# Memory attention of the second layer woven into the score levels of gated linear attention

## The chip, the cores and the metric

The kernel runs on one core of one Trainium2 chip (trn2). The metric is device time in microseconds (us) of one execution; lower is better. The program is written instruction by instruction: each engine (TensorE for matmuls, VectorE, ScalarE, GpSimd, and SyncE for DMA) runs its own list in order and waits on semaphores for the others.

## What is computed

The reference is one inference step of a two-layer decoder trunk, for one prompt of 256 tokens and for 8 batches of 4 sampled tokens (32 columns), so that activations are 288 columns wide. Layer 0 mixes tokens by native sparse attention, layer 1 by gated linear attention (GLA). Each layer also attends with 4 heads into 256 memory tokens, the prompt into keys and values computed here, each sampled batch into its own cached ones, and is followed by a squared-ReLU MLP. The part the change is about, for head h:

```python
def memory_attention(q, k, v, g_q, g_k):        # q (L, 128) of one head; k, v (256, 128)
    q = q * rsqrt(mean(q * q) + eps) * g_q      # norm of each query, gains per element
    k = k * rsqrt(mean(k * k) + eps) * g_k
    s = q @ k.T * 128 ** -0.5
    p = exp(s - max(s)); p = p / sum(p)
    return p @ v
```

In GLA the scores between tokens of a prompt are q(i) . k(j) times a decay exp(-sum of gates between j and i), per element of a 192-wide head. They are computed by levels: at level n, blocks of 2**n tokens are split in their middle, both factors are written relative to that middle, and a mask keeps the pairs whose common block has this size.

## The kernel before, in words

`linear_layer` (L2816) runs stages one after another; each is a block in which every engine has a list, and a block begins when all engines have ended the one before. Its stages are: the input projection, `prepare_linear`, `score_levels`, `linear_outputs` (L2476), then for the memory `normalize_queries` (L2719), `attend_memory_prompt` (L2757, which calls `attend_prompt`, L1370) and `attend_memory_sampled` (L2051), then `finish_linear` (L2667), after which the output projection follows.

`score_levels` (L2337) has 9 steps: levels 0 to 7, and a last one (CROSS, 8) for the pairs of the two halves of 128 tokens. For each level VectorE subtracts the decays (`diff`, L2377) two levels ahead, ScalarE takes Abs and Exp in place (L2424, L2426), VectorE multiplies the queries (L2387) and GpSimd the keys (L2436), TensorE multiplies the 4 heads (L2471), VectorE masks the result out of PSUM (L2399) and GpSimd adds it to `att` (L2444). A head of 192 elements takes two matmuls per product, one of 128 rows and one of 64. Every operand is float32, which TensorE runs in two passes, so the profile counts two records per matmul. Levels 0 to 2 also have the 32 sampled columns. The last step's copy is L2394.

`normalize_queries` squares the memory queries, sums over a head by a matmul with ones (L2734), takes the root and the reciprocal of the whole 128x1152 tile and multiplies. `attend_prompt` works on pairs of units (head, tile of 128 queries): scores (L1444), maximum (L1494, L1496), exponential (L1540), division (L1508), transposes (L1455), copy (L1557), output (L1465). `attend_memory_sampled` loads each batch's keys and values (L2088, L2089), squares (L2144, ScalarE), sums (L2177), roots, inverts, scales the keys on GpSimd (L2098), transposes them (L2110), copies (L2162), scores the 4 heads of a batch (L2120), and after a softmax multiplies the values (L2132).

In layer 0, `attend_sampled` (L1582) streams the cached keys and values of 40 chunks through slots: 10 in the weight ring (2 of them for keys) and 12 of its own (2 for keys).

Of the kernel before, what the change touches and what calls it, by code (L numbers as in the profile page):

```python
# [24 lines left out]
P = 128  # L25
# [641 lines left out]
def memory_keys_values(nc, g, a, base, layer, next_chunks):  # L667
# [3 lines left out]
    with ExitStack() as ctx:  # L671
# [77 lines left out]
        def _(dve):  # L749
# [29 lines left out]
            nc.vector.tensor_scalar(g.mem_k[layer], banks[:, 4:8, 0:MEM_LEN], g.vec[:, gk:gk + 1], None, ALU.mult)  # L779
# [11 lines left out]
def merge(*programs):  # L791

    ahead = [(next(p, None), n) for n, p in enumerate(programs)]
    while True:
        left = [(at, n) for at, n in ahead if at is not None]
        if not left:
            return
        n = min(left)[1]
        ahead[n] = (next(programs[n], None), n)

# [781 lines left out]
def attend_sampled(nc, g, a, base, next_chunks):  # L1582

    with ExitStack() as ctx:
# [10 lines left out]
        rest = sb("keys_values", [P, 12, CHUNK_PAGES, GROUPS * HD])  # L1595
# [3 lines left out]
        for n in range(TOTAL):  # L1599
# [6 lines left out]
            slots.append((region, at_ring, key_slot, 2 + list(before).index(v)))  # L1606
# [19 lines left out]
        pair_score = sb("pair_score", [P, PAIRS, 2 * CMP_BLOCKS // 2])  # L1626
# [10 lines left out]
        o = sb("o", [P, 2, HD])  # L1637
        k_ps = ps("k_ps", [P, GROUPS, 512])
# [258 lines left out]
        def _(dve):  # L1897
# [4 lines left out]
            def front():  # L1902
# [39 lines left out]
                nc.vector.tensor_reduce(pair_score[:], small_ps[:].rearrange("p (t n c) -> p t n c", t=PAIRS, c=2),  # L1942
# [394 lines left out]
def score_levels(nc, g):  # L2337

    CROSS = LEVELS
    with ExitStack() as ctx:
# [10 lines left out]
        ps = ctx.enter_context(nc.psum_tensor("lev_ps", [P, 2, GLA_HEADS, 512], F32))  # L2356
        diffed, distanced, exped, q_decayed, k_decayed, scored, masked, added = map(sem, (
            "diffed", "distanced", "exped", "q_decayed", "k_decayed", "scored", "masked", "added"))
# [8 lines left out]
        def blocked(ap, level):  # L2367
            return ap.rearrange("p k (n c) -> p k n c", c=2 ** level)

        @block.vector  # L2370
        def _(dve):
# [18 lines left out]
            def mask(level):  # L2390
                dve.wait_ge(scored, level + 1)
                src = ps[:, level % 2]
                if level == CROSS:
                    nc.vector.tensor_copy(g.att[:, :, 1], src[:, :, 0:P]).then_inc(masked, 1)  # L2394
                    return
# [3 lines left out]
                last = nc.vector.tensor_tensor(  # L2399
                    g.att[:, :, 0:3:2] if level == 0 else masked_to[level % 2],  # L2400
                    src[:, :, 0:SEQ].rearrange("p h (t i) -> p h t i", t=QT),
                    m.unsqueeze(1).unsqueeze(1).to_broadcast([P, GLA_HEADS, QT, P]), ALU.mult)
                if level in few_levels:
                    last = nc.vector.tensor_tensor(
                        g.att[0:SAMPLED, :, 3, 0:SAMPLED] if level == 0 else few[:, level % 2],
                        src[0:SAMPLED, :, SEQ:TOKENS],
# [3 lines left out]
            diff(1)  # L2410
            diff(2)
            for level in range(CROSS + 1):
                if level + 1 <= CROSS:
                    queries(level + 1)
                if level + 3 <= CROSS:
                    diff(level + 3)
                mask(level)

        @block.scalar
        def _(act):  # L2420
            for level in range(1, CROSS + 1):
                f = factor[level % 2][:, :, 0:span(level)]
                act.wait_ge(diffed, level)
                nc.scalar.activation(f, f, ACT.Abs).then_inc(distanced, 1)  # L2424
                act.wait_ge(distanced, level)
                nc.scalar.activation(f, f, ACT.Exp, scale=-1.0 / GATE_TAU).then_inc(exped, 1)  # L2426

        @block.gpsimd
        def _(pool):
# [20 lines left out]
            for level in range(1, CROSS + 1):  # L2450
                keys(level)
                if level >= 2:
                    add(level - 1)

        @block.tensor
        def _(pe):
            for level in range(CROSS + 1):
                lq, lk = (q, k) if level == 0 else (decayed_q[level % 2], decayed_k[level % 2])
                wait(pe, k_decayed, level)

                wait(pe, masked, level - 1)
                spans = [(slice(0, P), slice(P, SEQ), 0)] if level == CROSS else \
                    [(slice(t * P, (t + 1) * P), slice(t * P, (t + 1) * P), t * P) for t in range(QT)]
                if level in few_levels:
                    spans.append((slice(SEQ, TOKENS), slice(SEQ, TOKENS), SEQ))
                for h in range(GLA_HEADS):
                    for keys, queries, col in spans:
                        n = keys.stop - keys.start
                        pieces = head_pieces(h)
                        for e, (t, rows) in enumerate(pieces):  # L2470
                            mm = nc.tensor.matmul(ps[0:n, level % 2, h, col:col + n], lk[rows, t, keys],  # L2471
                                                  lq[rows, t, queries], start=(e == 0), stop=(e == len(pieces) - 1))
                mm.then_inc(scored, 1)
# [245 lines left out]
def normalize_queries(nc, g, layer, first):  # L2719

    with ExitStack() as ctx:
        sem = counters(nc, ctx, f"qnorm{layer}_")
        squares = ctx.enter_context(nc.sbuf_tensor(f"qnorm{layer}_squares", [P, MEM_HEADS, TOKENS], F32))
        gain = ctx.enter_context(nc.sbuf_tensor(f"qnorm{layer}_gain", [P, 1], F32))
# [226 lines left out]
```

## Time and profile before

| | us |
|---|---|
| median of 3 timed runs (lowest, highest) | 3810.02 (3807.48, 3811.71) |
| profiled execution, its own time | 3808.96 |
| its span, first to last instruction | 3806.7 |
| score levels (first product to the last copy's end) | 2489.95 to 2583.08 |
| the three memory stages of layer 1 | 2723.16 to 2812.41 |
| mean granted clock of TensorE over the span | 0.907 |

The span is divided into stages, and a stage's cost is read from the timeline between its first and its last instruction. A matmul record's time is as modelled from the granted clock; 1.00 of the windows' clock column is 2.4 GHz, 0.50 is 1.2 GHz, and values between are mixtures over the window.

### The profile page before, as it was taken

To read this page: it belongs to the slowest core of one execution; us is meant where nothing else is said; L and a number is where in the kernel's file an instruction comes from. 1 tells how busy PE (TensorE), PEld (TensorE's weight loads), DVE (VectorE), ACT (ScalarE), POOL (GpSimd) and SP (SyncE) were. 2 spreads that over 40 slices of the span, in tenths; PEclk is the share of its full clock that TensorE was granted. 3 is DMA by queue.
4 is the path that set the end of the run, shared out by engine and by line. 5 is a ranking of instruction groups with operands and counts; after the bars stand their busy time and mean duration, and the time that the engine had idled before them with its cause. 6 is when DMAs were issued, how large, how long until landed. Compare 5 with 4: busy or idle time off the path is not lost. (4 is left out here: it accounts for less than half of the span.)

```text
span 3806.7 us, 57145 instructions
## 1 busy us (share of the span) xinstructions
PE 3392.8 (89%) x23817; PEld 3088.4 (81%) x23817; DVE 1639.3 (43%) x1879; ACT 1274.9 (33%) x1363; POOL 208.7 (5%) x131
## 2 busy tenths in 40 slices
PE   7799999676577999999999999889759999999999
PEld 5699999354244999999999999863239999999999
DVE  4543334444544354333443354344544543334433
ACT  3432323123455243333333333230143433333322
POOL 0000000002231000000000000043010000000000
PEclk9899999656787999999999999957779999999999
DMA  4545352302554545454544444203245454445454
GB/s 143 185 159 173 117 158 92 117 1 89 166 188 142 164 149 164 146 166 155 166 154 164 160 155 165 85 1 112 100 144 166 144 165 150 165 160 164 148 166 136
DMA packets 317204, 537.06 MB, mean 141 GB/s; under 512 B 18213, under 2 KB 115455, under 8 KB 316040
## 3 DMA queue, kind: packets, MB, share of 16 engines
q1 hardware_dynamic: 316376, 529.70, 42.3%
q10 hardware_dynamic: 624, 4.46, 0.3%
q8 instruction: 150, 2.46, 0.3%
q14 instruction: 54, 0.44, 0.0%
HBM read 517.23 MB, written 25.19 MB: 142 GB/s over the span
## 5 line engine op out<-in xcount | busy, mean ns | idle before, releaser
L468 DVE TENSOR_TENSOR project_weights_low<-ring,project_weights_high 128x2048 fp32r<-128x2048 f32 x344 | 788.5, 2292 | 1203.0 <-ACT project_weights_high L403 1203.0
L403 ACT ACTIVATE project_weights_high<-ring 128x2048 fp32r<-128x2048 f32 x344 | 658.6, 1915 | 1264.3 <-PE project_banks L333 1264.2
L331 PE MATMUL project_banks<-high,project_weights_high 128*128 128x288 f32 x2560 | 763.3, 298 | 44.9 <-DVE project_weights_low L458 41.0
L332 PE MATMUL project_banks<-low,project_weights_high 128*128 128x288 f32 x2560 | 761.4, 297 | 0.0
L333 PE MATMUL project_banks<-high,project_weights_low 128*128 128x288 f32 x2560 | 761.2, 297 | 0.0
L331 PE MATMUL project_banks<-up_high,project_weights_high 128*128 128x288 f32 x2048 | 609.8, 298 | 27.5 <-DVE project_weights_low L458 27.5
L332 PE MATMUL project_banks<-up_low,project_weights_high 128*128 128x288 f32 x2048 | 608.7, 297 | 0.0
L333 PE MATMUL project_banks<-up_high,project_weights_low 128*128 128x288 f32 x2048 | 608.5, 297 | 0.0
L331 PEld LDWEIGHTS project_banks<-high,project_weights_high 128*128 128x128 f32 x2560 | 488.1, 191 | 47.3 <-DVE project_weights_low L458 42.6
L332 PEld LDWEIGHTS project_banks<-low,project_weights_high 128*128 128x128 f32 x2560 | 487.8, 191 | 0.0
L333 PEld LDWEIGHTS project_banks<-high,project_weights_low 128*128 128x128 f32 x2560 | 486.6, 190 | 0.0
L331 PEld LDWEIGHTS project_banks<-up_high,project_weights_high 128*128 128x128 f32 x2048 | 390.1, 190 | 28.4 <-DVE project_weights_low L458 28.4
L332 PEld LDWEIGHTS project_banks<-up_low,project_weights_high 128*128 128x128 f32 x2048 | 389.8, 190 | 0.0
L333 PEld LDWEIGHTS project_banks<-up_high,project_weights_low 128*128 128x128 f32 x2048 | 388.7, 190 | 0.0
L331 PE MATMUL project_banks<-project_high,project_weights_high 128*128 128x288 f32 x1088 | 322.6, 297 | 15.8 <-DVE project_weights_low L458 14.7
L333 PE MATMUL project_banks<-project_high,project_weights_low 128*128 128x288 f32 x1088 | 322.8, 297 | 0.0
L332 PE MATMUL project_banks<-project_low,project_weights_high 128*128 128x288 f32 x1088 | 322.3, 296 | 0.0
L949 PE MATMUL cmp_hid_ps<-cmp_blocks,ring 128*128 128x128 f32 (+1 forms) x2048 | 241.8, 276 | 0.0
L949 PEld LDWEIGHTS cmp_hid_ps<-cmp_blocks,ring 128*128 128x128 f32 x2048 | 236.4, 192 | 0.0
L331 PEld LDWEIGHTS project_banks<-project_high,project_weights_high 128*128 128x128 f32 x1088 | 206.0, 189 | 16.7 <-DVE project_weights_low L458 15.2
L332 PEld LDWEIGHTS project_banks<-project_low,project_weights_high 128*128 128x128 f32 x1088 | 206.1, 189 | 0.0
L333 PEld LDWEIGHTS project_banks<-project_high,project_weights_low 128*128 128x128 f32 x1088 | 205.9, 189 | 0.0
(422 smaller groups left out, 3347.2 us busy)
## 6 DMA issues: line engine op xcount, KB each, us to landing
ring<-in_w_up_dram SPq DMA_DIRECT2D x128, 1024.0 KB, 5.2
ring<-in_w_down_dram SPq DMA_DIRECT2D x128, 1024.0 KB, 5.1
ring<-in_gla_w_in_dram SPq DMA_DIRECT2D x40, 1024.0 KB, 5.0
h<-in_cache_nsa_kv_dram SPq DMA_DIRECT2D x256, 128.0 KB, 2.2
ring<-in_w_out_dram SPq DMA_DIRECT2D x32, 1024.0 KB, 5.1
ring<-in_nsa_w_in_dram SPq DMA_DIRECT2D x28, 1024.0 KB, 5.0
sp_keys_values<-in_cache_nsa_kv_dram SPq DMA_DIRECT2D x80, 256.0 KB, 3.5
ring<-in_w_mem_kv_dram SPq DMA_DIRECT2D x16, 1024.0 KB, 5.8
```

The source lines that it names most:

```text
L331: nc.tensor.matmul(bank, w_high, moving_high[:, kt], start=(kt == 0), stop=False)
L332: nc.tensor.matmul(bank, w_high, moving_low[:, kt], start=False, stop=False)
L333: mm = nc.tensor.matmul(bank, w_low, moving_high[:, kt], start=False, stop=(kt == k_tiles - 1))
L403: nc.scalar.activation(weights_high[:, c % 2], g.ring[:, c % RING], ACT.Copy).then_inc(rounded, 1)
L468: nc.vector.tensor_tensor(weights_low[:, c % 2], g.ring[:, c % RING], weights_high[:, c % 2].bitcast(F32), ALU.subtract).then_inc(split, 1)
L949: mm = nc.tensor.matmul(hid_ps[:, b % 2, m * HIDE_COLS:m * HIDE_COLS + hide_cols(b)], w1[:, j, m * P:(m + 1) * P], blocks[:, b % 2, j, 0:h ...
```

## The change

The three memory stages of layer 1 and their blocks are taken out. The same attention is issued inside the block of `score_levels`: each engine's list is a merge of two generators, which yield positions; the piece with the lower position is issued first. Memory positions (1 to 8 for the 8 units, 10.5 + hb/2 for 16 half batches of keys, 19 for the finish) are scaled by 9/22 to level positions.

- The norm of the queries is no longer multiplied into them: the factor goes into the exponential as its scale per row (`rms`, 9 columns), summed by 12 matmuls of one column. The queries' gain is in the memory keys instead: `mem_k` of layer 1 gets a second factor in its scaling instruction, the cached keys get it in the copy after the transposes.
- The units have one PSUM bank each for scores (a), transposes (b) and outputs (c); the keys are turned in banks a and c by halves (2 heads), and the scores of all batches gather in bank b.
- The levels have 4 banks for products instead of 8, 2 heads to a bank, in the order 0, 2, 1, 3, and one bank for the sampled columns, whose 8 matmuls come last in levels 0 to 2. The mask is two instructions of 128x512.
- The cached keys, then the values, go through 4 stage slots of 512 KB instead of 4 each with slots of their own; all scratch is in the weight ring.
- The values' product has the values stationary (128x128) and 4 columns moving: 8 matmuls a batch.
- In layer 0, `attend_sampled` has 13 slots of its own, 3 for keys, so 5 key slots in all.

```diff
@@ memory_keys_values
-            nc.vector.tensor_scalar(g.mem_k[layer], banks[:, 4:8, 0:MEM_LEN], g.vec[:, gk:gk + 1], None, ALU.mult)
+            nc.vector.tensor_scalar(g.mem_k[layer], banks[:, 4:8, 0:MEM_LEN], g.vec[:, gk:gk + 1],
+                                    g.vec[:, gq:gq + 1] if layer in MEM_RAW else 1.0, ALU.mult, ALU.mult)
@@ attend_sampled
-        rest = sb("keys_values", [P, 12, CHUNK_PAGES, GROUPS * HD])
+        rest = sb("keys_values", [P, 13, CHUNK_PAGES, GROUPS * HD])
...
-            key_slot = used[at_ring] % 2
+            key_slots = 2 if at_ring else 3
+            key_slot = used[at_ring] % key_slots
@@ score_levels
-        ps = ctx.enter_context(nc.psum_tensor("lev_ps", [P, 2, GLA_HEADS, 512], F32))
+        ps = ctx.enter_context(nc.psum_tensor("lev_ps", [P, 2, 2, 512], F32))
+        few_ps = ctx.enter_context(nc.psum_tensor("lev_few_ps", [P, 512], F32))
...
+        memory = memory_attention(nc, g, a, ctx, 1, GLA_MEM_Q, lambda m: m * (CROSS + 1) / MEM_STEPS)
...
+            def levels():                       # VectorE
+                diff(1)
+                diff(2)
+                for level in range(CROSS + 1):
+                    yield level
...
+                    yield level + 0.5
+                    mask(level)
+            merge(levels(), memory.vector(dve))
...
+                    yield level - 1.5           # ScalarE: Abs, Exp of a level
...
+                    yield level - 0.9           # GpSimd: keys of a level
...
+                        yield level - 0.4       # GpSimd: add of the level before
...
+                    for h in (0, 2, 1, 3):      # TensorE
+                        for keys, queries, col in spans:
+                            at = h // 2 * SEQ + col
+                            mm = product(ps[:, level % 2, h % 2, at:at + P], h, keys, queries)
...
+def memory_attention(nc, g, a, ctx, layer, first, at):
...
+    def loads(sp):
+        for n in range(2 * BATCH):
+            part, b = divmod(n, BATCH)
+            if n >= STAGES:
+                if n - STAGES < BATCH:
+                    sp.wait_ge(k_turned, 2 * (n - STAGES) + 2)
+                else:
+                    sp.wait_ge(out_done, U + n - STAGES - BATCH + 1)
+            sp.dma_start(stage[:, n % STAGES], rows[b, :, :, part]).then_inc(loaded[n % STAGES], 16)
...
+        def scores(u):
+            wait(pe, exped, u)
+            nc.tensor.matmul(bank_a[:, 0:MEM_LEN], q[:, k, i * P:(i + 1) * P], g.mem_k[layer][:, k], start=True,
+                             stop=True).then_inc(scored, 1)
...
+        def turn_keys(hb):
+            b, half = divmod(hb, 2)
+            if hb == 0:
+                pe.wait_ge(exped, U)
+            if hb == 1:
+                pe.wait_ge(out_copied, U)
+            pe.wait_ge(k_scaled, b + 1)
+            wait(pe, k_copied, hb - 1)
...
+            nc.scalar.activation(to, src[:, 0:MEM_LEN], ACT.Exp, bias=stat[:, u % 4, 0:1], scale=rms[:, col:col + 1],
+                                 accum_out=stat[:, u % 4, 1:2]).then_inc(exped, 1)
...
+            for u in range(U):                  # ScalarE
+                yield at(UNIT + u + 0.2)
+                exps(u)
+                if u:
+                    yield at(UNIT + u + 0.5)
+                    copies(u - 1)
...
+            for hb in range(-5, HB):            # ScalarE
+                b, half = divmod(hb, 2)
+                yield at(at_half(hb))
+                if hb >= 0:
+                    copy_keys(hb)
+                if half and 0 <= b + 3 < BATCH:
+                    square(b + 3)
+                if not half and 0 <= b + 2 < BATCH:
+                    root(b + 2)
@@ linear_layer
-            score_levels(nc, g)
+            score_levels(nc, g, a)
             linear_outputs(nc, g, a)
-        normalize_queries(nc, g, 1, GLA_MEM_Q)
-        attend_memory_prompt(nc, g, 1, g.p, GLA_MEM_Q)
-        attend_memory_sampled(nc, g, a, 1, g.p[:, GLA_MEM_Q:GLA_MEM_Q + MEM_HEADS, SEQ:TOKENS],
-                              g.h[:, HEADS:KT, SEQ:TOKENS])
```

The lists as the two programs issue them. TensorE before, levels 3 to 5 (L2471 is the products of a level; a row ends with its number of instructions):

```order
L2471 MATMUL lev_ps<-lev_decayed 128x128 x16
L2471 MATMUL lev_ps<-h 128x128 x16
L2471 MATMUL lev_ps<-lev_decayed 128x128 x16
```

TensorE after, from level 3 (the first L2499) to level 5 (the last). L2596 is a unit's scores, L2604 its transposes, L2613 its output, L2628 the transposes of half a batch's keys, L2641 their scores:

```order
L2499 MATMUL lev_ps<-lev_decayed 128x128 x16
L2613 MATMUL mem_bank_c<-ring,mem_v 128x128 x2
L2596 MATMUL mem_bank_a<-mem_k,gla_projected 128x256
L2604 MATMUL mem_bank_b<-ident,ring 128x128 x2
L2613 MATMUL mem_bank_c<-ring,mem_v 128x128 x2
L2604 MATMUL mem_bank_b<-ident,ring 128x128 x2
L2613 MATMUL mem_bank_c<-ring,mem_v 128x128 x2
L2499 MATMUL lev_ps<-h 128x128 x16
L2628 MATMUL mem_bank_a<-ident,ring 128x128 x4
L2628 MATMUL mem_bank_c<-ident,ring 128x128 x4
L2641 MATMUL mem_bank_b<-ring 32x256 x2
```

Where two levels followed each other directly, the rest of the units now stands between levels 3 and 4, and from level 4 on the keys.

ScalarE after, around the Abs (L2446) and Exp (L2448) of level 5; before, these two instructions followed each other with nothing between levels. L2698 and L2705 are a unit's exponential and copy, L2711 the squares, L2716 the root, L2724 the copy of half a batch:

```order
L2698 ACTIVATE ring,mem_stat<-mem_bank_a,mem_stat,mem_rms 128x256
L2705 ACTIVATE ring<-mem_bank_b 128x256
L2716 ACT_TABLE_LOAD
L2716 ACTIVATE mem_ss<-mem_ss 128x8
L2446 ACTIVATE gla_projected<-gla_projected 128x6x256
L2448 ACT_TABLE_LOAD
L2448 ACTIVATE gla_projected<-gla_projected 128x6x256
L2711 ACTIVATE ring<-ring 128x1024
L2705 ACTIVATE ring<-mem_bank_b 128x256
L2716 ACT_TABLE_LOAD
L2716 ACTIVATE mem_ss<-mem_ss 128x8
```

The last unit's copy (the second L2705) stands behind the first root, a level's Abs and Exp, two table loads and a square. In the whole block ScalarE loads a table 10 times.

## Rows read from the trace of the kernel before

**Rows 1.** The page, its first section: busy time, share of the span, instructions.
```profile
PE 3392.8 (89%) x23817; PEld 3088.4 (81%) x23817; DVE 1639.3 (43%) x1879; ACT 1274.9 (33%) x1363; POOL 208.7 (5%) x131
```

**Rows 2.** Windows of the levels, the stage removed, its first loads.
```profile
2502.00:2583.00 81.00, 79.83 (x272) 56.14 (x272) 32.28 (x25) 17.80 (x12) 50.02 (x16) 0.50 0.00 1
2723.00:2813.00 90.00, 43.67 (x331) 29.51 (x331) 38.09 (x99) 32.69 (x56) 19.35 (x14) 0.73 0.26 94
2762.00:2775.00 13.00, 0.37 (x2) 0.41 (x3) 5.28 (x17) 4.79 (x6) 4.59 (x3) 0.63 0.87 317
```

**Rows 3.** Timeline of the levels: start us, us, engine, line, out<-in, [idle before].
```profile
2501.88 13.59 PE L2471 MATMUL lev_ps<-lev_decayed 128*128 128x128 f32 x48
...
2548.32 9.92 PE L2471 MATMUL lev_ps<-lev_decayed 128*128 128x128 f32 x32
...
2550.49 0.51 PEld L2471 LDWEIGHTS lev_ps<-lev_decayed 64*128 64x128 f32 x4 [0.22 <-issue]
...
2552.66 0.93 PEld L2471 LDWEIGHTS lev_ps<-lev_decayed 128*128 128x128 f32 x4 [0.22 <-issue]
...
2582.39 0.69 DVE L2394 COPY gla_att<-lev_ps 128x512 f32<-128x512 f32 x1 [2.54 <-PE lev_ps L2471]
```

**Rows 4.** Groups by line and shape, window 2440 to 2860.
```profile
L2377 DVE TENSOR_TENSOR gla_projected<-gla_decay 128x1536 f32<-128x1536 f32 x6 | 10.6, 1759 | 31.3 <-POOL h L2436 15.7 <-POOL lev_decayed L2436 15.7
L2436 POOL TENSOR_TENSOR lev_decayed<-gla_projected 128x1536 f32<-128x1536 f32 x3 | 10.3, 3418 | 0.0
...
L2424 ACT ACTIVATE gla_projected<-gla_projected 128x1536 f32<-128x1536 f32 x6 | 8.9, 1483 | 46.8 <-DVE gla_projected L2377 46.8
```

**Rows 5.** Timeline at the edges of the stage removed.
```profile
2719.91 0.46 DVE L2643 TENSOR_TENSOR gla_projected<-gla_projected,linout_swish 128x288 f32<-128x288 f32 x1
2723.16 0.15 DVE L2746 TENSOR_SCALAR qnorm_gain<-vec 128x1 f32<-128x1 f32 x1 [2.79 <-PEq L2479]
...
2805.97 5.37 PE L2132 MATMUL mem_o_ps<-ring,mem_probs 128*32 128x128 f32 x128 [0.97 <-DVE mem_probs L2196]
...
2812.70 3.36 ACT L2696 ACTIVATE gla_projected<-h 128x864 f32<-128x864 f32 x4 [8.77 <-PEq L2054]
...
2813.67 2.69 PE L2689 MATMUL fin_ps<-gla_projected,ones 128*128 128x288 f32 x10 [1.59 <-ACT gla_projected L2696]
```

**Rows 6.** Timeline of two units of the prompt's memory attention.
```profile
2740.11 1.28 ACT L1540 ACT_TABLE_LOAD   x1 [9.11 <-PEq L2721]
...
2744.66 1.06 PE L1444 MATMUL memory_s_ps<-mem_k,memory_q 128*128 128x256 f32 x2
...
2745.76 0.42 DVE L1494 TENSOR_REDUCE memory_maxima<-memory_s_ps 128x1 f32<-128x256 f32 x1 [1.64 <-PE memory_s_ps L1444]
...
2746.41 0.47 ACT L1540 ACTIVATE memory_probs<-memory_s_ps,memory_maxima 128x256 f32<-128x256 f32 x1 [1.12 <-DVE memory_maxima L1496]
...
2747.80 0.38 ACT L1557 ACTIVATE memory_turned<-memory_t_ps 128x256 f32<-128x256 f32 x1 [0.83 <-PE memory_t_ps L1455]
...
2748.32 0.64 PE L1465 MATMUL memory_o_ps<-memory_turned,mem_v 128*128 128x128 f32 x4
2748.52 0.42 DVE L1494 TENSOR_REDUCE memory_maxima<-memory_s_ps 128x1 f32<-128x256 f32 x1 [1.29 <-PE memory_s_ps L1444]
```

**Rows 7.** Timeline of one sampled batch's keys.
```profile
2774.63 1.94 PE L2110 MATMUL mem_k_ps<-ident,mem_stage 128*128 128x128 f32 x8 [12.86 <-POOL mem_stage L2098]
...
2777.71 1.05 ACT L2144 ACTIVATE mem_squares<-mem_stage 128x1024 f32<-128x1024 f32 x1
...
2778.94 0.64 PE L2120 MATMUL mem_s_ps<-mem_turned_k,mem_q 128*32 128x256 f32 x8
```

**Rows 8.** DMA issues of the window 2755 to 2815.
```profile
mem_stage<-in_cache_mem_kv_dram SPq DMA_DIRECT2D x8, 512.0 KB, 4.4
```

**Rows 9.** Timeline of ScalarE in sparse attention.
```profile
1118.68 0.68 ACT L1851 ACTIVATE sp_turned_k<-sp_k_ps,vec 128x512 f32<-128x512 f32 x1
...
1176.50 1.06 ACT L1838 ACTIVATE mem_k<-sp_keys_values 128x1024 f32<-128x1024 f32 x1 [1.69 <-DMA sp_keys_values<-in_cache_nsa_kv_dram]
```

More of the change, by code:

```diff
@@ L797, in merge @@
             return
-        n = min(left)[1]
+        at, n = min(left)
+        yield at
         ahead[n] = (next(programs[n], None), n)
+def merge(*programs):
+    for _ in ordered(*programs):
+        pass
 def page_chunks(a, g, kind, stage, loaded):
@@ L2368, in blocked, with _ @@
             return ap.rearrange("p k (n c) -> p k n c", c=2 ** level)
+        @block.sync
+        def _(sp):
+            for _ in memory.loads(sp):
+                pass
         @block.vector
@@ L2391, in mask @@
                 dve.wait_ge(scored, level + 1)
[L2392 removed]
+                src = [ps[:, level % 2, b].rearrange("p (h n) -> p h n", h=2) for b in range(2)]
                 if level == CROSS:
[L2394 removed]
+                    for b in range(2):
+                        last = nc.vector.tensor_copy(g.att[:, b:GLA_HEADS:2, 1], src[b][:, :, 0:P])
+                    last.then_inc(masked, 1)
                     return
@@ L2448, in add, with levels @@
                 last.then_inc(added, 1)
[L2450 to L2453, printed above, removed]
+            def levels():
+                for level in range(1, CROSS + 1):
+                    yield level - 0.9
+                    keys(level)
+                    if level >= 2:
+                        yield level - 0.4
+                        add(level - 1)
+            merge(levels(), memory.gpsimd(pool))
@@ L2455, in _, with levels, product @@
         @block.tensor
         def _(pe):
[L2457 to L2468, printed above, removed]
+            def levels():
+                for level in range(CROSS + 1):
+                    yield level
+                    lq, lk = (q, k) if level == 0 else (decayed_q[level % 2], decayed_k[level % 2])
+                    wait(pe, k_decayed, level)
+                    wait(pe, masked, level if level in few_levels else level - 1)
+                    spans = [(slice(0, P), slice(P, SEQ), 0)] if level == CROSS else \
+                        [(slice(t * P, (t + 1) * P), slice(t * P, (t + 1) * P), t * P) for t in range(QT)]
+                    def product(out, h, keys, queries):
@@ L2469, in _ @@
                         pieces = head_pieces(h)
                         for e, (t, rows) in enumerate(pieces):
-                            mm = nc.tensor.matmul(ps[0:n, level % 2, h, col:col + n], lk[rows, t, keys],
-                                                  lq[rows, t, queries], start=(e == 0), stop=(e == len(pieces) - 1))
-                mm.then_inc(scored, 1)
+                            last = nc.tensor.matmul(out, lk[rows, t, keys], lq[rows, t, queries], start=(e == 0),
+                                                    stop=(e == len(pieces) - 1))
```

339 lines of the change are left out of this document (282 added, 57 removed).

## The prediction

> **What bounds the kernel now.** I read the page first: TensorE is busy 89% of the span [rows 1]. A share over the whole span says nothing of a stage, so next I cut windows. In the score levels TensorE is busy 79.83 of 81 us, VectorE 32.28, ScalarE 17.80 and GpSimd 50.02, and the granted clock is 0.50, the 1.2 GHz level [rows 2]. In the memory stages that are removed TensorE is busy 43.67 of 90 us at 0.73; of these 90, 13 go by with 0.37 us of TensorE work, while the first loads run at 317 GB/s [rows 2]. The two stages look complementary: one is full on TensorE, the other nearly empty. But both are one chain: while levels run, only the other engines have room, and memory attention needs TensorE three times per unit. So I read the timeline for what a level's products cost [rows 3], the groups for what the level loop costs elsewhere [rows 4], the edges of the removed stages [rows 5], and one unit and one batch for their chains [rows 6, 7].
>
> **What is removed.** The last VectorE instruction ahead of the stages ends at 2720.37, their first starts at 2723.16, and the next stage's first ScalarE instruction starts at 2812.70 [rows 5]. The next stage would have started some 2.3 to 2.8 us after 2720.37, as theirs did. 2812.70 - 2723.16 = 89.5; I take -90.0, with the small differences between what starts first in a block.
>
> **The level products themselves.** From level 3 a level is 16 matmuls, 9.92 us [rows 3]. The weight loads of most come singly, and three times per level two are loaded together (x4 records, once of 64 and once of 128 partitions are shown): 16 - 3 = 13 steps of 0.76 us, most spaced 0.72. The rows of 64 partitions pair where one head ends with the lower half of a tile and the next head starts with an upper half. In the order 0, 2, 1, 3 this happens once, not twice, and two heads that share a bank cannot be relied on to run beside each other: 15 steps of 0.72 = 10.85, so +0.93 in each of levels 3 to 7 (+4.7) and +1.1 in the last. Levels 1 and 2 take 13.59 now [rows 3] with the sampled columns between; with them gathered, 10.85 and 8 short matmuls, some 13.0: -1.2 to -1.5 together. Level 0 starts now at a higher clock, right behind other matmuls, and would start behind a wait for squares: +1.5. Sum +6, bounds 0 (all pairs kept) and +12 (every step single).
>
> A rule of the Trainium skill bears on the keys and values here: "TensorE: Matmul & The Clock Gate", Part 3, says that matmuls of few output columns on distinct column groups of the array run concurrently. The trace agrees: 128 records of 32 columns for the values take 5.37 us, 0.042 each [rows 5], the scores of four heads 0.64 for 8 records [rows 7]. The change leaves two groups for the scores and none for the values, so the rule speaks against it; by it the values alone would cost four times 5.37, by column count four moving columns instead of 128 take most of it back.
>
> **What is added, by gaps.** In the new list TensorE runs a level and then a few memory pieces, each of which waits for another engine, so the block gets longer by the gaps between levels. ScalarE is the engine behind most of them.
>
> A unit: scores start at 2744.66 and end 1.06 later at the slow clock, the maximum starts at 2745.76 (0.42), the exponential at 2746.41 (0.47, and reading its sum 0.19), a copy of the transposes 0.38, an output 0.64 to 1.06 [rows 6]. Before, a unit starts every 2.76 (2745.76 to 2748.52) with two in flight. Now there is one bank of each kind, and the copy of unit u-1 stands behind the exponential of unit u: scores 1.06, to the end of the exponential 1.25 and 0.3 for its sum, copy 0.38, output 0.9: 3.9, say 4.0 (3.0 at full clock).
>
> - Ahead of level 0: square of 128x1152 on ScalarE and 12 matmuls of one column: 3.1.
> - After level 0 (scores, scores, transposes): 1.06 + 1.6 + 1.06 + 0.7 and hand-overs = 4.7.
> - After levels 1 and 2: two outputs more than whole units, 8.9 and 9.3, each near 2.3 periods.
> - After level 3: the last pieces of three units 6.2, then the last output, whose copy on ScalarE stands behind root, Abs, Exp, a square and two table loads of 1.28 [rows 6]: of 2 x 1.28 + 2 x 1.48 + 1.05 + 0.2 = 6.8 [rows 4, 6, 7] some 5.8 is open. 12.0.
> - A half batch: 4 transposes at the slow clock are half of 1.94 to 1.97 for eight records, times two records each and so 1.0 to 1.5; a copy of 512 columns 0.68 [rows 9]; scores on two column groups 0.3 to 0.6. With the ends of the waits 2.4. ScalarE has per level 5 x 0.68, 2.5 x 1.05 and 2 x 1.48 + 2 x 1.28 = 11.5 beside them, a little under level and gap together. So level 4 (three and a half of them): 9.6; level 5: 12.6; level 6: 11.3; level 7, two and a half left: 4.3.
> - Tail behind the last level: transposes, copy (some 1.7), 64 matmuls of 4 columns, 128 records. No row has their shape: 32 stationary columns take 0.042 each [rows 5], 128 moving ones 1.94 / 8 = 0.243 [rows 7]. I take 0.073, near the first since few columns move: 9.3 (ends 5.4 and 31). The value loads of batches 4 to 7 wait for slots that the products of 0 to 3 free and land 4.4 us later [rows 8], which opens 3 us more: 14.0 (10.1 to 36).
>
> Together 3.1 + 4.7 + 8.9 + 9.3 + 12.0 + 9.6 + 12.6 + 11.3 + 4.3 + 14.0 = 89.8. Bounds: all pieces ready when TensorE comes to them (their own matmul time only: 43.67 of the removed stages [rows 2], dearer by the lost column groups: some 55) and, above, each of the 8 gaps and the tail 2.5 us longer, 112 (and 22 more by the tail's far end, which I give next to no weight). I keep 89.8: the nearest row is the unit's, and it is a chain.
>
> What of it lies beside the levels: the loads, squares, sums and scalings (1.05 ScalarE, GpSimd scaling) and the unit norms; what lies on the path is above. The level loop's other side, subtraction 1.76, Abs and Exp 2 x 1.48, keys 3.42 [rows 4], fits in level plus gap, about 20 us, so no level waits for its operands.
>
> **The rest.** Clock: with gaps between them the levels may be granted 1.00 in places, as units were (0.73 over the removed stages [rows 2]); half a level saved, -5, bounds 0 and -25 (five levels at half their time). The next stage: its first matmuls took 2.69 for 10 [rows 5] right behind other TensorE work; behind `linear_outputs` and a barrier they start slower, +2.3 (bounds 0, +5). Five key slots: ScalarE waits for key loads before its squares here and there (1.69 before that at 1176.50 [rows 9], eight such waits, 7.7 in all), two of them really for value slots; at most -5.1, I take -3.5, and 0 if the loads are limited by the queue. The second factor in `mem_k`'s scaling is free: same instruction; above, 0.2.
>
> Sum: -90.0 + 6 + 89.8 - 5 + 2.3 - 3.5 = -0.4. Against the profiled execution's 3808.96 that is 3808.6; the median of the runs stands 1.1 higher, 3809.6. As errors of gaps with slack on the other side are more often towards overlap (a piece that was ready), I round down: 3808.
>
> **Rivals.** (1) The weave pays: TensorE finds pieces ready because ScalarE and VectorE do them during the 10 us of a level, and one or two stretches are granted the full clock. For it: VectorE is busy 32 and ScalarE 18 of 81 us [rows 2], ScalarE waits 46.8 of them for the subtraction [rows 4]. Against: only one unit is in flight. Each gap loses about one hand-over chain (2 us, 16) and the clock gives 12 instead of 5: 3808 - 23 = 3785; with more of the clock 3775.
> (2) The other side: ScalarE's list. Its Abs and Exp wait for a subtraction that waits for GpSimd's keys, and everything of memory attention behind them waits too: exponentials, copies, squares. One wait of 2 us in each of 8 gaps is +16: 3824. It decides when ScalarE's waits for the subtraction, 46.8 now, stand in the middle of memory pieces; it is harmless as long as the subtraction is done when ScalarE comes to it, which levels of 20 us instead of 10 favour.
> (3) The table loads. There are ten of 1.28 each [rows 6]; if each also has to empty ScalarE's pipe and costs as much again, and six of ten stand on the path, +8 to +13: 3819. The Trainium skill, "ScalarE: Activation LUTs", What ACT_TABLE_LOAD costs, puts such a switch at about 2.66 us, a drain and a load; row 2740.11 has 1.28 and shows nothing of a drain.
>
> **How the numbers follow.** A change of 0.2% (7.6 us) is about what a measurement of this kernel can tell. Forecast (near 3808, own range 3799 to 3819) 0.43, of which 0.08 ends faster, 0.33 within, 0.02 slower; (1) 0.30, all faster; (2) 0.18, slower; (3) 0.09, 0.02 of it within. Faster 0.38, same 0.35, slower 0.27. The range that leaves 0.1 out on each side is 3778 to 3827.
>
> **What would show it.** Between the end of one level's products and the first of the next (L2499 rows) the gaps above, 9 to 13 us in the middle; levels of 10.85 at clock 0.50; the longest gap after level 3 with ScalarE as releaser; from the block's first product to its last copy 93.1 + 6 + 89.8 - 5 = 184 us. A block under 165 says rival 1, and the windows tell whether by clock or by gaps; over 195 with ScalarE waiting for L2389 in the gaps says rival 2; ScalarE idle right at table loads says rival 3. The forecast is wrong if a level waits for its keys, or if sparse attention moves by over 5 us either way.

## The result, and where the time went

The changed kernel takes 3826.72 us (median of 6 runs, 3822.33 to 3833.15) against 3810.35 (3805.44 to 3814.05, 6 runs): a ratio of 1.0049, 95% interval 1.0038 to 1.0060. It is slower by 16 us by the medians (14 to 23 by the interval), where 3808 and no measurable change were forecast. The profiled execution took 3822.33, its span is 3820.4, 13.7 more than before. The page, where [rows 1] had 3392.8 us:

```profile
PE 3421.8 (90%) x23832; PEld 3112.3 (81%) x23832; DVE 1637.7 (43%) x1870; ACT 1282.9 (34%) x1379; POOL 196.9 (5%) x126
```

TensorE is busy for 29 us more, although the number of its instructions hardly moved. The timeline of TensorE in the changed kernel, the block's start, the gap after level 3 and the tail (L2499 is a level's products, the answer to L2471 in [rows 3]; L2683 the sampled values):

```profile
2484.21 2.63 PE L2647 MATMUL mem_bank_c<-ones,ring 128*128 128x1 f32 x16 [1.96 <-ACT ring L2752]
2486.99 10.93 PE L2499 MATMUL lev_ps<-gla_projected 128*128 128x128 f32 x32
...
2550.57 10.77 PE L2499 MATMUL lev_ps<-lev_decayed 128*128 128x128 f32 x32
2561.13 1.06 PE L2613 MATMUL mem_bank_c<-ring,mem_v 128*128 128x128 f32 x4
2561.98 1.06 PE L2596 MATMUL mem_bank_a<-mem_k,gla_projected 128*128 128x256 f32 x2
2562.83 0.63 PE L2604 MATMUL mem_bank_b<-ident,ring 128*128 128x128 f32 x2
2564.77 0.71 PE L2613 MATMUL mem_bank_c<-ring,mem_v 128*128 128x128 f32 x4 [1.30 <-ACT ring L2705]
2565.59 0.44 PE L2604 MATMUL mem_bank_b<-ident,ring 128*128 128x128 f32 x2
2571.67 1.22 PE L2613 MATMUL mem_bank_c<-ring,mem_v 128*128 128x128 f32 x4 [5.64 <-ACT ring L2705]
2572.69 10.77 PE L2499 MATMUL lev_ps<-h 128*128 128x128 f32 x32
...
2654.29 3.00 PE L2499 MATMUL lev_ps<-h 128*128 128x128 f32 x16
2657.12 0.38 PE L2673 MATMUL mem_bank_a<-ident,ring 128*128 128x128 f32 x2
2657.98 26.25 PE L2683 MATMUL mem_bank_c<-ring 128*128 128x4 f32 x128 [0.47 <-ACT ring L2705]
...
2684.86 1.19 PE L2948 MATMUL linout_o_ps<-gla_att,gla_v_rows 128*128 128x256 f32 x2 [0.63 <-PEq L2350]
```

The rows between two L2499 rows are memory pieces; a bracket is idle time, and in this gap ScalarE's L2705, the copy of a unit's transposes, ends both waits. The last but one row is the result: 128 records with 4 columns moving take 26.25 us, and TensorE is never idle in it, since the row has no break.

The windows of the same tail say at which clock (us, busy times by engine, granted clock, DMA share, GB/s):

```profile
2654.50:2658.00 3.50, 3.03 (x19) 2.07 (x18) 1.74 (x6) 1.04 (x3) 0.00 (x0) 1.00 0.36 135
2658.00:2661.00 3.00, 3.00 (x20) 3.00 (x21) 0.08 (x1) 0.00 (x0) 0.00 (x0) 0.73 0.00 0
2661.00:2670.00 9.00, 9.00 (x43) 9.00 (x44) 0.00 (x0) 0.00 (x0) 0.00 (x0) 0.50 0.54 167
```

The last level ran at 1.00, the value product started there, and the clock fell to 1.2 GHz within its first 3 us (0.73 over them is 1.4 us at 1.00 and the rest at 0.50) and stayed. PE and PEld are busy alike; that the time is the loading of 128x128 stationary values is tested below.

From ends of stages on TensorE and VectorE in both traces the balance is:

| | forecast | measured |
|---|---|---|
| up to the end of layer 1's input projection (sparse attention's slots) | -3.5 | -6.9 (2449.86 to 2443.01) |
| ahead of level 0 | +3.1 | +3.9 |
| the levels themselves, clock included | +6 - 5 | +3.6 (92.4 to 96.0) |
| the 8 gaps | +72.7 | +74.3 |
| tail behind the last level | +14.0 | +26.5 |
| stages removed | -90.0 | -89.6 |
| linear_outputs, the stage after it, the rest | +2.3 | +1.9 |
| sum | -0.4 | +13.7 |

### The profile page after: what moved, and what is told of

It is laid out like the page before. It is cut to its first block and busy times, and to the rows that moved or that the text cites. A ratio compares the mean times of both kernels' runs of the same rounds, so it can differ in the third digit from the quotient of the medians.

```text
span 3820.4 us, 57170 instructions
## 1 busy us (share of the span) xinstructions
PE 3421.8 (90%) x23832; PEld 3112.3 (81%) x23832; DVE 1637.7 (43%) x1870; ACT 1282.9 (34%) x1379; POOL 196.9 (5%) x126
## 5 line engine op out<-in xcount | busy, mean ns | idle before, releaser
L331 PE MATMUL project_banks<-up_high,project_weights_high 128*128 128x288 f32 x2048 | 610.6, 298 | 27.5 <-DVE project_weights_low L458 27.5
```

The source lines that it names most:

```text
L331: nc.tensor.matmul(bank, w_high, moving_high[:, kt], start=(kt == 0), stop=False)
```

## Experiments

All intervals are against the kernel before on the same chip. The differences from the changed kernel compare separate measurements, in which the median of the kernel before lies between 3807.75 and 3810.35; so they are good to some 3 us, and those of a single run are less sure. A name such as "tail" is the stretch from the last level's products to the first of the next stage. A line "..." in an edit stands for lines left out.

**More columns moving.** To see what a record of the value product costs:

```diff
-    mm = nc.tensor.matmul(bank_c[:, cols], stage[:, n % STAGES, t, h * HD:(h + 1) * HD],
-                          turned[:, t * P + cols.start:t * P + cols.stop],
+    mm = nc.tensor.matmul(bank_c[:, h * 64:(h + 1) * 64], stage[:, n % STAGES, t, h * HD:(h + 1) * HD],
+                          turned[:, t * P:t * P + 64],
```

> The changed kernel with 64 columns moving instead of 4 in the 64 matmuls of the sampled values (the product then means nothing; it leaves the rest alone). Theory L (a record costs what its 128x128 stationary load costs, 0.205 us at the 1.2 GHz level, whatever moves): the 128 records stay at 25 to 28 us. Rival D (TensorE waits for the value loads of batches 4 to 7): also 26, so this run does not tell D. Rival M (short matmuls cost by their moving columns plus a fixed part): 60 more columns in two passes add at least 60 x 2 / 1200 = 0.1 us a record, 13 us in all, 39.

Measured: 3811.24 in its one run, 15.5 less than the changed kernel's median, and no theory had it. Sixteen times the columns take 11.7 us less. Its timeline, then its windows:

```profile
2655.03 14.58 PE L2683 MATMUL mem_bank_c<-ring 128*128 128x64 f32 x128 [0.47 <-ACT ring L2705]
```

```profile
2650.00:2655.00 5.00, 4.33 (x27) 2.47 (x26) 1.78 (x6) 1.73 (x4) 1.14 (x1) 1.00 0.34 105
2663.00:2670.00 7.00, 6.61 (x59) 6.47 (x58) 0.29 (x1) 0.00 (x0) 0.00 (x0) 1.00 0.39 143
```

The product starts at 1.00 as before, but with 64 columns it stays there: 14.58 / 128 = 0.114 us a record, against 26.25 / 128 = 0.205. The 0.205 is a mean that holds the first 1.4 us at 1.00; a run further down has the same product at 0.50 throughout, 27.47 / 128 = 0.215. This fits one cost that scales with the clock and hardly with the moving columns. So theory L held for what a record is made of, and missed the clock.

**Fewer stationary columns.**

```diff
-                    mm = nc.tensor.matmul(bank_c[:, cols], stage[:, n % STAGES, t, h * HD:(h + 1) * HD],
+                    mm = nc.tensor.matmul(bank_c[0:32, cols], stage[:, n % STAGES, t, h * HD:h * HD + 32],
```

> The changed kernel with the first 32 columns of each head's values stationary instead of 128 (three quarters of the output are left out), 4 columns moving as before. Theory L: the load of 32 columns is a quarter, so the 128 records fall from 26.2 to between 6 and 10 us unless the value loads then show (up to 4.4 us of landing behind batch 3's slot). Rival D (waits for the loads) and rival F (a fixed time per instruction on TensorE's queue): they stay above 20.

Measured: 3810.9 in its one run. The tail of its timeline:

```profile
2665.61 1.02 PE L2683 MATMUL mem_bank_c<-ring 128*32 128x4 f32 x16 [1.86 <-DMA ring<-in_cache_mem_kv_dram]
...
2668.07 1.02 PE L2683 MATMUL mem_bank_c<-ring 128*32 128x4 f32 x16 [0.26 <-DMA ring<-in_cache_mem_kv_dram]
```

A batch's 16 records take 1.02 us, 0.064 each, under a third of 0.215 at the same low clock; now TensorE does wait for value loads. The whole product took 11 us (2658.0 to 2669.1), waits included. The stationary operand's columns are the cost; rivals D and F fall.

**Without the last four loads.** In this kernel the loads of values 4 to 7 are not issued:

```diff
-        for n in range(2 * BATCH):
+        for n in range(2 * BATCH - STAGES):
...
-            pe.wait_ge(loaded[n % STAGES], 16 * (n // STAGES + 1))
+            pe.wait_ge(loaded[n % STAGES], 16 * (BATCH // STAGES + 1))
```

> The changed kernel without the value loads of batches 4 to 7; their products read the slots as batches 0 to 3 left them. Theory L: no change, 26 us for the 128 records. Rival D (the landing of four loads of 512 KB is in the 26.2 us): 3 us or more less.

Its product, in its timeline:

```profile
2655.88 26.15 PE L2683 MATMUL mem_bank_c<-ring 128*128 128x4 f32 x128 [0.47 <-ACT ring L2705]
```

26.15 for 26.25, and 3823.74 in its one run, inside the changed kernel's range. The prediction's "which opens 3 us more" for the landing was wrong as well: a product this slow covers the loads.

**The slots alone,** on the kernel before:

```diff
-        rest = sb("keys_values", [P, 12, CHUNK_PAGES, GROUPS * HD])
+        rest = sb("keys_values", [P, 13, CHUNK_PAGES, GROUPS * HD])
...
-            key_slot = used[at_ring] % 2
+            key_slots = 2 if at_ring else 3
+            key_slot = used[at_ring] % key_slots
...
-        pair_score = sb("pair_score", [P, PAIRS, 2 * CMP_BLOCKS // 2])
...
+        pair_score = o[:].rearrange("p a d -> p (a d)").rearrange("p (t n) -> p t n", t=PAIRS)
```

> The kernel before with only the five key slots of sparse attention added. The trace of the changed kernel has attend_sampled 9.3 us shorter and the stages around it 4 longer, gated linear attention starting 6.9 earlier. Theory: the slots alone give 5 to 9 us, 3801 to 3805. Rival (the prediction's): at most 5.1 by the waits of ScalarE's squares, 3805 to 3808. Rival (run to run difference of the granted clock): nothing.

Measured: 3803.10 (11 runs) against 3808.91, ratio 0.9984, interval 0.9975 to 0.9993: 6 us, between 3 and 10. In its profile `attend_sampled` is 242.1 long instead of 253.3, the stages ahead of it 2.6 longer. The prediction's upper bound, 5.1, counted only ScalarE's waits for key loads; the stage gained 11 here (9.3 in the changed kernel). The queue of loads shows where. Waits of SyncE's queue over sparse attention in the kernel before, for key slots to be turned (L1702, L1706):

```profile
SPq L1702 <- PE sp_k_ps L1754: 45.4, 14, 6.1
SPq L1706 <- PE sp_k_ps L1754: 18.5, 4, 7.3
```

and with the slots:

```profile
SPq L1703 <- PE sp_k_ps L1755: 19.2, 5, 7.3
SPq L1707 <- PE sp_k_ps L1755: 5.6, 3, 4.3
```

63.9 us of queue waiting became 24.8. One queue issues keys and values in order, so a key load that waited for its slot also held up the value loads behind it, which no wait of ScalarE's squares names. That this is the missing half is my reading; no run separated it.

**The weave alone,** the changed kernel with four key slots (and 12 slots of its own again, although the expectation speaks of a thirteenth):

```diff
-        rest = sb("keys_values", [P, 13, CHUNK_PAGES, GROUPS * HD])
+        rest = sb("keys_values", [P, 12, CHUNK_PAGES, GROUPS * HD])
...
-            key_slots = 2 if at_ring else 3
+            key_slots = 2
```

> The changed kernel with two key slots in the ring and two of its own, four in all, as before (the thirteenth slot holds values that nothing waits for): the weave alone. The traces have the woven block 18.7 us over the blocks that it replaces; with the slots' 5 to 9 us taken off the result: 3828 to 3834. Rival (slots give nothing once the weave is there): as the changed kernel, 3826.

Measured: 3831.66 (4 runs), ratio 1.0064, interval 1.0048 to 1.0079: the weave costs 18 to 30 us, and the slots hid a part of it. `attend_sampled` is back at 252.6, and the value product at 26.22.

**Values on column groups,** as the kernel before had them, in the woven block (`own_probs` takes the place of dead scratch, zeroed by GpSimd; eight copies place the probabilities):

```diff
+            for t in range(QT):
+                for h in range(MEM_HEADS):
+                    mm = nc.tensor.matmul(bank_c[32 * h:32 * h + 32, 0:HD], own_probs[:, t, h, b],
+                                          stage[:, n % STAGES, t, h * HD:(h + 1) * HD], start=(b == 0 and t == 0),
+                                          stop=(b == BATCH - 1 and t == QT - 1), skip_group_check=True)
```

> The changed kernel with the values product as the kernel before had it: probabilities placed in zeroed blocks of 32 columns are stationary on four column groups, the values move; still through four slots, so batches 4 to 7 load behind the products of 0 to 3. Theory L (128 full stationary loads made the tail 26 us): the 128 records take 5 to 7 us of work, spread over 9 to 12 by the landing of the last loads; with eight small copies, a copy and a transposition added (2 us), the time falls by 12 to 15 us, to 3812 to 3815. Rival D: the product falls little, above 3822.

Measured: 3809.17 (10 runs, 3803.93 to 3818.59), ratio 1.0001, interval 0.9991 to 1.0010, so some 18 us under the changed kernel's ratio, more than the 12 to 15 expected. The last part of its product:

```profile
2665.66 1.08 PE L2691 MATMUL mem_bank_c<-ring 128*32 128x128 f32 x16 [4.14 <-DMA ring<-in_cache_mem_kv_dram]
2667.12 2.24 PE L2691 MATMUL mem_bank_c<-ring 128*32 128x128 f32 x32 [0.39 <-DMA ring<-in_cache_mem_kv_dram]
```

16 records of four heads take 1.08 at the slow clock, 0.068 each, and the 4.14 us wait for the fifth batch's values stands where the forecast had put 3 us for the landing. Two things changed here at once: the stationary operand has 32 columns instead of 128, and four heads stand on four column groups. The run with 32 stationary columns and no groups had 0.064 with 4 columns moving, so the narrow operand accounts for the price; that 128 moving columns cost next to nothing more may be the groups' doing, which no run separates. The product as a whole went from 26.2 to 11.0 us. The profiled execution is the slowest of its ten, and it shows a long stretch in another stage:

```profile
2776.70:2807.40 30.70, 30.70 (x54) 6.31 (x52) 11.18 (x15) 0.00 (x0) 2.01 (x2) 0.50 0.34 115
```

`linear_outputs` has here a stretch of 30.7 us at 0.50; the changed kernel has 0.76 over the same window, its clock going up and down. The stage takes 145.1 instead of 137.5. What decides it was not settled; the other profile with the values on column groups (all three edits, below) has 145.0 too, and none of the others is over 139.9.

**Abs and Exp beside the levels.**

```diff
-                    yield level - 1.5
+                    yield level - 1.0
```

> The changed kernel with Abs and Exp of each level half a level earlier in ScalarE's list, so that they run beside the products of a level and not among the memory pieces of a gap. Theory A (the longest waits in the gaps, 5.6, 2.6, 3.6 and 3.0 us, stand behind Abs, Exp and their table loads): gaps after levels 3 to 6 fall by 2 to 5 us each, 8 to 13 us in all, 3814 to 3819. Rival (subtraction and keys come late for the queries then, or the same wait moves to another piece): within 3 us of the changed kernel.

Measured: 3804.81 (10 runs), ratio 0.9991, interval 0.9981 to 1.0000: 22 us under the changed kernel, more than the 8 to 13 expected. ScalarE in the gap after level 3, in the changed kernel:

```profile
2564.34 0.37 ACT L2705 ACTIVATE ring<-mem_bank_b 128x256 f32<-128x256 f32 x1
2564.73 1.28 ACT L2716 ACT_TABLE_LOAD   x1
...
2566.03 0.21 ACT L2716 ACTIVATE mem_ss<-mem_ss 128x8 f32<-128x8 f32 x1
2566.14 1.47 ACT L2446 ACTIVATE gla_projected<-gla_projected 128x1536 f32<-128x1536 f32 x1
2567.63 1.28 ACT L2448 ACT_TABLE_LOAD   x1
2568.92 1.48 ACT L2448 ACTIVATE gla_projected<-gla_projected 128x1536 f32<-128x1536 f32 x1
2570.31 1.04 ACT L2711 ACTIVATE ring<-ring 128x1024 f32<-128x1024 f32 x1
2571.26 0.36 ACT L2705 ACTIVATE ring<-mem_bank_b 128x256 f32<-128x256 f32 x1
```

From one copy to the next 6.9 us, all of it other work of ScalarE; here TensorE waits its 5.64. With the edit the chain is short:

```profile
2562.81 0.21 ACT L2716 ACTIVATE mem_ss<-mem_ss 128x8 f32<-128x8 f32 x1
...
2562.93 1.04 ACT L2711 ACTIVATE ring<-ring 128x1024 f32<-128x1024 f32 x1
2563.87 0.36 ACT L2705 ACTIVATE ring<-mem_bank_b 128x256 f32<-128x256 f32 x1
```

The gap after level 3 falls from 11.4 to 7.2 and the one after level 6 from 12.1 to 7.5. Those after levels 4 and 5 do not fall: other waits came in, behind VectorE's copy of the last unit's output and behind GpSimd's scaling of keys, as the rival had it.

```profile
2581.35 1.11 PE L2628 MATMUL mem_bank_c<-ident,ring 128*128 128x128 f32 x4 [4.43 <-DVE h L2784]
...
2602.78 1.12 PE L2628 MATMUL mem_bank_a<-ident,ring 128*128 128x128 f32 x4 [4.46 <-POOL ring L2588]
```

All eight gaps go from 74.3 to 65.5, -8.8. The number is the expected one, but theory A holds for two gaps of four: the waits after levels 3 to 6 fell by only 2.7 us together, and most of the rest is memory pieces that ran at a higher clock. The levels gained by the clock as well: two were granted 1.00 throughout. In its windows levels 5, 6 and 7:

```profile
2586.20:2592.50 6.30, 6.30 (x36) 4.61 (x35) 2.90 (x4) 4.93 (x6) 3.17 (x2) 1.00 0.23 83
2604.80:2615.70 10.90, 10.90 (x35) 7.74 (x34) 3.53 (x4) 4.65 (x5) 6.35 (x3) 0.50 0.00 0
2623.20:2629.50 6.30, 6.30 (x35) 4.58 (x34) 1.76 (x1) 4.40 (x4) 2.23 (x1) 1.00 0.32 86
```

The same products take 6.3 us or 10.9. The sum of the levels is 86.9 instead of 96.0. Why these two levels and not the one between them got the full clock is not shown. The sampled values' product, unchanged in this run, began at 0.50 and stayed there (0.50 over 2637.2 to 2664.6):

```profile
2637.13 27.47 PE L2683 MATMUL mem_bank_c<-ring 128*128 128x4 f32 x128 [0.47 <-ACT ring L2705]
```

**Heads in order.**

```diff
-                    for h in (0, 2, 1, 3):
+                    for h in range(GLA_HEADS):
```

> The changed kernel with the heads of a level in the order 0, 1, 2, 3. Theory O (pairs of weight loads run side by side where heads follow each other in different banks, three pairs a level instead of one): a level from 3 on falls from 10.8 to 9.9 us, all of them together by 6 to 8 us, 3819 to 3821. Rival: within 2 us.

Measured: 3811.08 (10 runs), ratio 1.0004, interval 0.9992 to 1.0015: 15 to 17 us under the changed kernel. Each level of 10.8 takes 9.8, the nine together 87.3 for 96.0 (8.7, a little over the 6 to 8 expected); the whole profiled execution is 12 us shorter. That is the 9.92 of the kernel before [rows 3]. A level's weight loads (PEld) merge in three rows of four again, where the changed kernel has one, at 2555.47:

```profile
2548.05 0.51 PEld L2499 LDWEIGHTS lev_ps<-lev_decayed 64*128 64x128 f32 x4 [0.22 <-issue]
...
2550.23 0.93 PEld L2499 LDWEIGHTS lev_ps<-lev_decayed 128*128 128x128 f32 x4 [0.22 <-issue]
...
2552.83 0.51 PEld L2499 LDWEIGHTS lev_ps<-lev_decayed 64*128 64x128 f32 x4 [0.23 <-issue]
```

The order changes both which half tiles are neighbours and which neighbours share a bank; no run tells these two apart. The remaining few us of the time are not explained; two of the ten runs were at 3797.

**All three.**

> The three edits of these runs together (values moving on four column groups, Abs and Exp half a level earlier, heads in the order 0 to 3). If they add up: 26 to 36 us less than the changed kernel, 3791 to 3801, and faster than the kernel before. If one hides another's gain (a shorter level leaves ScalarE less cover): 3802 to 3808.

Measured: 3787.82 (5 runs, 3782.80 to 3791.37), ratio 0.9946, interval 0.9932 to 0.9959: 15 to 26 us faster than the kernel before, 39 less than the changed kernel and under the 3791 to 3801 that were expected. The block is 163.1 long from first level to the next stage, against 197.9. The single gains (18, 22 and 16, together 56) are more than this. In the traces the levels take 78.9 instead of 96.0, the gaps 68.0 instead of 74.3, the tail 16.2 instead of 27.6, and `linear_outputs` 145.0 instead of 137.5. By how much the single gains share the clock's part was not taken apart.

**The product kept warm.** 64 columns again, now so that the product is right: those of a head pair move, the four that count are copied out of four banks.

```diff
+                to, pair = b % 2 * 256 + h * 64, h // 2 * 64
...
+                    mm = nc.tensor.matmul(value_banks[b // 2][:, to:to + 64], stage[:, n % STAGES, t, h * HD:(h + 1) * HD],
+                                          turned[:, t * P + pair:t * P + pair + 64],
```

> The changed kernel with the values product computed for 64 probability columns (those of a pair of heads) instead of the 4 of the batch, into four PSUM banks; the 4 that mean something are copied out. Theory C (with 4 columns the granted clock falls 1.4 us into the product, with 64 it stays at 1.00, and a record costs its stationary load at that clock): 128 records in 14 to 15.5 us, the time 10 to 14 us under the changed kernel, 3812 to 3816. Rival (the single run with 64 columns was luck of the clock): the product at 0.2 us a record or more, 26 us, no gain.

Measured: 3812.45 (10 runs), ratio 1.0007, interval 0.9998 to 1.0017: 14 us under the changed kernel by the medians (16 by the ratios), as theory C had it. Its product takes 14.9 us in all; its first half:

```profile
2659.42 3.79 PE L2685 MATMUL mem_bank_c<-ring 128*128 128x64 f32 x32 [0.47 <-ACT ring L2707]
2663.04 3.74 PE L2685 MATMUL mem_bank_b<-ring 128*128 128x64 f32 x32
```

**Warm product with the other two edits.**

> Wide values product, Abs and Exp half a level earlier, heads in the order 0 to 3. If the product stays at 1.00: 14.6 us in place of the 12 that the column groups took with waits, but a warm stage behind it (137 to 140 us instead of 145): 3784 to 3790, level with or under the run of all three. Rival (the clock at the tail depends on where the levels end): the product at 26 us, 3796 or more.

Measured: 3797.83 (6 runs, 3789.86 to 3807.42), ratio 0.9967, interval 0.9954 to 0.9979. The median is the rival's outcome; the fastest run reaches 3789.86. Only the slowest of the six, 3807.42, has a profile:

```profile
2638.29 7.09 PE L2685 MATMUL mem_bank_c<-ring 128*128 128x64 f32 x32 [0.47 <-ACT ring L2707]
2645.17 7.03 PE L2685 MATMUL mem_bank_b<-ring 128*128 128x64 f32 x32
```

```profile
2633.00:2638.00 5.00, 4.04 (x18) 2.85 (x18) 2.96 (x6) 0.81 (x3) 3.03 (x2) 0.64 0.24 91
2645.00:2655.00 10.00, 10.00 (x49) 10.00 (x48) 0.77 (x8) 0.00 (x0) 0.00 (x0) 0.50 0.49 150
```

The levels end at another moment, the clock is at 0.50 when the product begins, and with 64 columns it stays there: 27.6 us, 0.215 a record. So the 64-column product stayed in each profile at the clock at which it began, 1.00 in two of them and 0.50 in this one; what the five other runs had is not known. The kernel with all three edits is 10 us faster by the medians, though the two intervals overlap a little; its values product took less than half of this one at the same clock, waits included.

## Why the prediction was wrong

**The step that failed** is the price of a record in the tail: "128 moving ones 1.94 / 8 = 0.243 [rows 7]. I take 0.073, near the first since few columns move: 9.3 (ends 5.4 and 31)". Measured was 0.205, 26.25 us, near the far end "which I give next to no weight". The two rows that it stands between were misread: both have 128 columns moving, and they differ in stationary columns (32 in [rows 5], 128 in [rows 7]), besides the column groups and the clock (0.66 and 0.50 over them). The change has 128 stationary columns, so its row was the second. The runs say the same: 32 stationary columns instead of 128 take the record from 0.215 to 0.064 at the low clock; 64 moving columns instead of 4 take nothing at that clock (0.215 both). The product is 26.25 against 9.3 + 3, so +14, of a total miss of 14 in the profiled runs (18.7 by the median, against 3808). The rest nearly cancels: the tail's other pieces cost 1.4 less and the slots gave 3.4 more, while the levels cost 2.6 more, the gaps 1.6 and the start 0.8.

**The second half of it is the clock.** The forecast does not say at which clock its 0.073 holds. The 64-column product at the fast clock took 14.58, 5.3 more than 9.3; so the price was too low at either clock, and the fall 1.4 us into the product is the other 11.7 of the 26.25.

**The rule that spoke against the change** was read and then set aside. The Trainium skill ("TensorE: Matmul & The Clock Gate", Part 3) says that matmuls of few output columns on distinct column groups run concurrently. The prediction's "four times 5.37" by it is 21.5 us, and it went on: "four moving columns instead of 128 take most of it back". They took back nothing that the runs show. How much the groups themselves are worth here stays open: 16 records take 1.08 us with four groups and 1.02 with none, both with 32 stationary columns, and 16 x 0.215 = 3.4 with 128.

**What held.** The block by gaps: 72.7 forecast, 74.3 measured; after level 3 12.0 and 11.4, its one long wait 5.8 and 5.64; after levels 4 and 5 9.6 and 12.6, measured 9.6 and 12.5. Level products of 10.85 were 10.8 to 10.9. Removal -90.0 was -89.6.

**What held by luck.** The agreement of the gaps from level 4 on is partly luck. The forecast had a steady 2.4 us per half batch, with 0.3 to 0.6 for its scores, and ScalarE's list hidden under level and gap. In the trace, at the slow clock, the scores take 1.07 and half a batch 2.0 of TensorE's own time, and each gap after levels 4 to 6 has one wait of 2.6 to 3.6 us for a copy (L2724) that stands behind Abs and Exp. Over the block TensorE is idle for 26 us only; the larger part of the 74.3 is its own matmuls, not the chain.

**What failed beside it.** The prediction called itself wrong "if sparse attention moves by over 5 us either way", and `attend_sampled` became 9.3 shorter: the bound of 5.1 went by the wrong engine's waits. The 5 us that the clock was to give back on the levels were some 2.4, in the last one only: 3.00 us at 1.00, against half of 10.85.

**The rivals.** (1) A paying weave is not seen in this kernel. With the three edits the time comes out as this rival had it, but by other means in part: of its terms, the gaps lost 6.3 us and the clock gave some 8 on two levels, while the tail lost 11.4 and the order of the heads 8.7. (2) ScalarE waiting for subtraction: its waits for L2389 add up to 0.8 us in the block, where they were 46.8 before. The block came out at 197 us, over the 195 that were this rival's sign, but by the tail. (3) Table loads: the rows of the gap after level 3 show each at 1.28, with work before and after closing up to 0.03 us; nothing of a second cost. The Trainium skill ("ScalarE: Activation LUTs", What ACT_TABLE_LOAD costs) puts a switch at 2.66 us, a load and a drain; these rows have the load alone.

## What to carry to other kernels

When a matmul is turned around so that the large operand is stationary, price it by its stationary columns per record, and take the row for that from an instruction with as many of them: here 4 and 64 moving columns cost the same at the same clock. Look up which of a row's numbers are the stationary ones before two rows are compared. Give the price at both clocks, since the clock of the stretch is not known ahead. When work is woven into a block, write down each engine's list around one gap: the piece that the gap waits for belongs ahead of everything that only the next step needs; then look which wait ends last next, since it can take the place of the first. And check an order of heads that was made for one reason for what ran side by side in the old one.

## What the runs showed of the hardware

- float32 records with 128x128 stationary: 0.215 us at the 1.2 GHz level, with 4 columns moving (27.47 / 128) as with 64 (27.56 / 128); 0.114 at the 2.4 GHz level with 64. With 32 stationary columns and 4 moving 0.064 at the low level.
- The value product with 4 columns moving began at 1.00 and was at 0.50 after 1.4 us, with PE and PEld busy without a break; with 64 columns moving it stayed at 1.00 for 14.6 us. Begun at 0.50, it stayed there with 4 columns (27.5 us) and with 64 (27.6 us). What decides this was not settled.
- Level products that fill TensorE without a break ran at 0.50 in most levels, 10.9 us, and at 1.00 in two levels of the kernel with Abs and Exp earlier, 6.3 us. What decides it was not settled.
- Ten table loads in the block take 1.28 us each; ScalarE's instruction before each of them ends 0.02 us ahead of it.
